# Interleaving the high and low half of each weight block in the expert matmuls of a hybrid decoder layer

## What is computed

```python
def expert(acc, prm):
    wg, wu, wd, gt = prm
    hid = jax.nn.silu(h @ wg) * (h @ wu)
    return acc + gt[:, None] * (hid @ wd), None

out, _ = lax.scan(expert, jnp.zeros_like(h), (w_gate, w_up, w_down, gates.T))
```

## Time and profile before

| | us |
|---|---|
| median of 3 runs | 792.75 (791.99 to 793.56) |
| span of the profiled execution | 794.2 |
| PE busy in it | 728.8 (92%) |
| PE weight loads | 570.3 (72%) |
| DVE busy | 636.6 (80%) |
| ACT busy | 526.4 (66%) |
| POOL busy | 307.2 (39%) |

### The profile page before, as it was taken

One profiled execution on the slowest core, in us unless ns is written; L12 is line 12 of the kernel. 1 busy time (PEld: TensorE's weight loads), 2 busy tenths in 40 slices (PEclk: granted clock), 3 DMA queues, 4 the chain that ended last, 5 costly groups with the idle time before them and its releaser, 6 DMA issues.

```text
span 794.2 us, 12672 instructions
## 1 busy us (share of the span) xinstructions
PE 728.8 (92%) x4733; PEld 570.3 (72%) x4734; DVE 636.6 (80%) x538; ACT 526.4 (66%) x544; POOL 307.2 (39%) x214
## 2 busy tenths in 40 slices
PE   3669999989679999999999999999999999999980
PEld 1248577544457888888888888888888888888860
DVE  3363294635648999999999999999999999999973
ACT  2020133455527887888888888878888888888761
POOL 7300000040053456654456644566544566544000
PEclk9979999999659999999999999999999999999996
DMA  8999987710528899999999999999999999999501
GB/s 337 357 405 379 367 313 275 292 69 0 212 76 309 319 383 378 372 367 370 383 379 364 377 371 372 381 381 369 372 373 381 365 383 369 371 375 372 202 0 61
DMA packets 102004, 249.78 MB, mean 315 GB/s; under 512 B 8134, under 2 KB 8146, under 8 KB 98898
## 3 DMA queue, kind: packets, MB, share of 16 engines
q1 hardware_dynamic: 96448, 244.33, 82.9%
q10 hardware_dynamic: 5092, 3.46, 1.4%
q0 software_dynamic: 432, 1.59, 0.6%
HBM read 248.30 MB, written 1.07 MB: 314 GB/s over the span
## 4 chain that ended last, share of the span: by engine, by line
PE 84%; DVE 5%; DMA 4%; POOL 2%; ACT 2%; issue 2%; ACTq 0%; DVEq 0%; POOLq 0%
PE PS L1250 45%; PE PS L1238 8%; PE PS L1218 7%; PE PS L1209 6%; PE PS L1042 5%; PE PS L1160 3%; PE PS L1036 3%; POOL line L373 2%; DMA toe<-line_dram 2%; PE PS L1228 1%; DMA tabT<-in_rel_bias_dram 1%; PE PS L1017 1%; DVE MOD L698 1%; DVE S L774 1%; DVE S L754 1%
## 5 line engine op out<-in xcount | busy, mean ns | idle before, releaser
L918 DVE TENSOR_TENSOR WL<-W,WH 128x2048 fp32r<-128x2048 f32 x187 | 419.8, 2295 | 7.1 <-ACT WH L619 7.1
L619 ACT CAST WH<-W 128x2048 fp32r<-128x2048 f32 x187 | 349.9, 1903 | 48.6 <-PE PS L1250 48.6
L416 POOL TENSOR_SCALAR OG<-slot_no,cur 128x128 f32<-128x128 f32 x64 | 161.7, 2531 | 0.0
L1250 PE MATMUL PS<-WH,XT 128*128 128x512 f32 x512 | 140.2, 396 | 0.6 <-DVE XT L928 0.6
L1250 PE MATMUL PS<-WL,XT 128*128 128x512 f32 x508 | 140.0, 397 | 0.0
L403 POOL COPY cur<-PG 128x4 f32 (+1 forms) x33 | 8.3, 251 | 274.8 <-PE PS L1228 227.3
L1250 PEld LDWEIGHTS PS<-WH,XT 128*128 128x128 f32 x512 | 97.0, 190 | 23.8 <-DVE XT L928 0.6
L1250 PEld LDWEIGHTS PS<-WL,XT 128*128 128x128 f32 x508 | 96.0, 189 | 22.4
L413 POOL TENSOR_SCALAR OH<-slot_no,cur 128x128 bf16<-128x128 f32 x64 | 106.5, 1674 | 0.0
L1250 PE MATMUL PS<-WH,HT 128*128 128x512 f32 x256 | 70.5, 398 | 1.5 <-issue 1.5
L698 DVE SCALAR_TENSOR_TENSOR MOD<-W,cS,MOD 128x2048 f32<-128x2048 f32 x20 | 46.9, 2347 | 30.1 <-DMA W<-in_w_ada_dram 29.8
(11 more groups left out here) (184 smaller groups left out, 762.3 us busy)
## 6 DMA issues: line engine op xcount, KB each, us to landing
W<-in_w_gate_dram SPq DMA_DIRECT2D x64, 1024.0 KB, 8.0
W<-in_w_down_dram SPq DMA_DIRECT2D x64, 1024.0 KB, 6.2
W<-in_w_up_dram SPq DMA_DIRECT2D x63, 1024.0 KB, 9.9
W<-in_w_ada_dram SPq DMA_DIRECT2D x24, 1024.0 KB, 8.1
W<-in_w_in_dram SPq DMA_DIRECT2D x12, 1024.0 KB, 13.2
W<-in_w_out_dram SPq DMA_DIRECT2D x4, 1024.0 KB, 11.6
toe<-line_dram POOLq DMA_DIRECT2D x1, 1536.0 KB, 14.5
X<-in_x_dram ACTq DMA_DIRECT2D x1, 1024.0 KB, 12.4
```

The costliest lines, as they stand in the source:

```text
L416: nc.gpsimd.tensor_scalar(OG[:, buf, t, :], slot_no[:], cur[:, buf, 0, t:t + 1], cur[:, buf, 1, t:t + 1], ALU.is_equal, ALU.mult).then_inc ...
L619: nc.scalar.copy(WH[:, (UPE * odd + u) % SPLITS, :], source).then_inc(hi_ready, 1)
L918: nc.vector.tensor_tensor(low, source, WH[:, (UPE * odd + u) % SPLITS, :].bitcast(f32), ALU.subtract).then_inc(lo_ready, 1)
L1250: last = nc.tensor.matmul(PS[:, bank, :], lhsT, w[:, q * 512:(q + 1) * 512], start=begin, stop=end)
```

## The change

In `unit` both waits, on `hi_ready` and on `lo_ready`, now stand ahead of the first matmul. The loop over the four blocks is now outside, and the loop over the high and the low half inside: the block from WH and the same block from WL follow each other, and both go past the same stationary block. The matmuls are the same in number, shape and destination. The last one still raises `split_used`. Nothing on ACT, DVE, POOL or SP changes.

```diff
                 def unit(n, at, spare, outs):
 
-                    for high in (True, False):
-                        pe.wait_ge(hi_ready if high else lo_ready, n + 1)
-                        w = WH[:, at % SPLITS, :] if high else (HnL if spare else WL[ring_slot(0, at)])[:]
-                        for q in range(4):
+                    pe.wait_ge(hi_ready, n + 1)
+                    pe.wait_ge(lo_ready, n + 1)
+                    for q in range(4):
+                        for high in (True, False):
+                            w = WH[:, at % SPLITS, :] if high else (HnL if spare else WL[ring_slot(0, at)])[:]
                             bank, lhsT, begin, end = outs(q, high)
                             last = nc.tensor.matmul(PS[:, bank, :], lhsT, w[:, q * 512:(q + 1) * 512],
                                                     start=begin, stop=end)
```

## The result

The changed kernel takes 815.64 us (815.14 to 817.90) against 793.15 us (791.99 to 794.59) for the kernel before, four runs each: a ratio of 1.028, with a 95% interval of 1.025 to 1.031. It is 22.5 us slower; 20.2 us had been forecast. The profiled execution has a span of 813.6 us. The kernel before was run again beside the experiments, with medians of 793.35 us (e1 to e4) and 794.49 us (e5 to e7); the ratios given with them are to those runs, and are not the plain quotients of the medians.

A forecast was written before the change was run, and what follows sets the result against it. PE was taken as the bound, with DVE close behind; 0.69 + 0.07 - 0.12 = 0.64 us a turn over 31 turns, plus 0.36, gave 20.2 us on the 792.75 us median: 813.0 us, range 809 to 822.

The forecast's parts named there:

- What bounds the kernel, and where: Expert pass: PE busy throughout each 16.82 us turn, DVE nearly so; moving the wait costs 0.64 us a turn at unit 3.
- the cover of unit 3: Unit 3's four high-half matmuls, under which DVE finishes the low half, 0.69 us after PE has started the unit.
- The delay stays: DVE's next start follows PE's end of unit 3 by a slackless 3.33 us chain, so the offset returns every turn.
- The hand-over: Time from DVE's end of unit 3's low half to PE's load: taken as 0.07 us, bounds 0.05 and 0.23.
- The catch-up: Unit 3 after its wait: first four loads take 0.76 us and not 0.88, giving back 0.12 us; other bound nothing.
- The last expert's unit 5: `hidden(31)` stands ahead of its low half, so PE waits there: 0.41 + 0.07 - 0.12 = 0.36 us, once.
- Sharing a stationary block: High and low matmuls on one stationary block: saves between nothing and 0.01 us per four matmuls; taken as nothing.
- The extra wait ahead of a unit: Second wait before each unit's first load: made good by PE's queue; at unit 4 perhaps a few hundredths of a microsecond.
- The wait paid once: Rival: DVE gains 0.64 us on PE in the first turn and keeps it; 793.4 us, no change; chance 0.03.
- the fall of the clock: Rival: PE's new idle time each turn lowers its clock, 31 x 1.6 = 50 us more, 863 us; chance 0.05.
- the gain from shared blocks: Rival: wait paid once and matmuls shorter, up to 0.12 us a turn, 3.7 us in all; 789.7 us; chance 0.03.
- The sum: Whole kernel: 31 x 0.64 = 19.8, and 0.36: 20.2 us slower, 813.0 us for the median.

The follow-up runs named there:

- e1: Changed kernel with the old matmul order (four blocks from WH, then four from WL), both waits still ahead of the unit: 816.85 us, ratio to before 1.029.
- e4: Changed kernel, PE's code untouched, with unit 3's high half made ahead of YH on ACT and its low half ahead of YL on DVE: 797.34 us, ratio 1.0035.
- e5: Changed kernel with unit 3's halves made ahead of YH and YL, and only the wait on `lo_ready` ahead of a unit: 793.60 us, ratio 0.9996.
- e7: Kernel before, PE's order and waits kept, with only unit 3's halves made ahead of YH and YL: 794.38 us, ratio 1.0002.
- two single-part runs: e1, the moved wait without the new matmul order, 816.85 us; and e2, the new order without unit 3's moved wait, 794.55 us.
- e2: Changed kernel, but unit 3 and the last expert's unit 5 keep the old order and old place of the wait: 794.55 us, ratio 1.001.
- e6: Changed kernel with only the wait on `lo_ready` ahead of a unit, ACT and DVE in their old order: 813.78 us, ratio 1.024.

## Why the prediction was right

- *What bounds the kernel, and where.* Right. PE was the bound by its busy time, with DVE close behind; the cover of unit 3 was the place. The wait occurs at unit 3 in 31 turns and at unit 5 of the last expert, and nowhere else is a low half waited for. The two single-part runs show the wait to be the whole cost and the order to be none of it.
- *The delay stays.* Right. The loop as now measured over turns 3 to 28: DVE's start to the end of unit 3's low half 11.93 us (11.90 forecast), hand-over 0.12 (0.07), load of unit 3 to ACT's copy 2.16 (2.16), copy to DVE's next start 3.33 (3.33); 17.53 us in all against 17.46.
- *The hand-over* is the term that was mis-sized most. The bounds were 0.05 and 0.23 us, and I took 0.07 on the ground that the load would carry the wait. With two waits ahead of the load only one of them rides on it in this trace, and the one on the low half is an instruction of its own (L1246, 51 ns): 0.12 us. With one wait it is 0.05 us. That is 0.05 us a turn, 1.5 us of the 2.3 us that the forecast fell short of. DVE's part, 0.02 us longer, is 0.7 us more.
- *The catch-up* after a wait was right: 0.34 us from the first load to the second matmul against 0.46 in the stream, 0.12 us.
- *The last expert's unit 5* was put at 0.36 us and cost 0.41: its second matmul starts at 790.24, and one distance of 0.23 after another from 789.37 would have had it at 789.83.

```profile
789.37 0.40 PE L1251 MATMUL PS<-WL,HT 128*128 128x512 f32 x1
...
790.24 0.39 PE L1251 MATMUL PS<-WL,HT 128*128 128x512 f32 x1
```

- *Sharing a stationary block.* Right in that it saves nothing that counts: 4734 loads as before. In the five kernels with the alternating order in which no wait falls inside a unit (after, e2, e4, e5, e6) the mean distance between two matmuls of a unit is 230.7 to 231.9 ns, for 231.9 before, hence at most 1.2 ns a matmul. The scatter was not the only such pair in the kernel before: in units 4 and 5 two blocks in a row already share their stationary block (`k = 2 * (u - 4) + q // 2`), and the distance inside such a pair is no shorter there (232.5 ns on the mean, 232.1 from one pair to the next). The 216 ns that the Trainium skill gives in "TensorE: Matmul & The Clock Gate" ("Back-to-back issue gap"), as the isolated gap of a matmul of 512 columns, were not reached by any of the five, and the 131 ns that it gives there for a sustained stream less still; the distance after the first matmul of a pair is the same as after the second, within 1 ns.
- *The extra wait ahead of a unit* "may add a few hundredths of a microsecond, which end in the wait at unit 3". Both halves hold: it is 0.08 us at unit 4, unseen in the changed kernel, and it showed as soon as the wait at unit 3 was removed.
- *The rivals.* The wait paid once is refuted by the even turns; the fall of the clock did not come (1.00 through the turns); the gain from shared blocks is bounded above.
- *The sum.* 31 x 0.716 + 0.41 = 22.6 us, for 22.5 measured. The interval of the ratio stands for 19.8 to 24.4 us, so that an agreement within 0.1 us is luck; what the terms are worth is known from the traces.
- *One reading was wrong, without effect.* The prediction puts the profiled span of 794.2 us 1.45 us above the median of the runs. But the median is of launch times, which are longer than the span: 815.3 us for a span of 813.6 in the profiled execution of after. By that difference of 1.7 us the profiled execution of the kernel before lay nearly 3 us above the median, an estimate. The forecast for the median does not use the difference.

## What to carry to other kernels

When a step that was interleaved with its inputs is changed to need all inputs at its start, look up for each instance when the last input arrives and compare it with the start of the step, not with its present use: here five of six units had margins of 0.84 us and more, and the sixth had none. Then ask whether the engine that is late gets its own next start from the engine that now waits; if it does, the delay is paid in every turn, however idle the late engine becomes. A second wait ahead of an instruction is not free where the engine is late already: here it cost 0.06 us at unit 3 and 0.08 us at unit 4. Wait on the one semaphore that implies the other.

## What the hardware showed beyond that

With unit 3's low half ahead of YL, POOL's OG instructions (L416) took 3.81 us on the mean in place of 2.75, and POOL was busy for 113 us in ten turns in place of 92. POOL's work is the same; what changed is what DVE does beside it, four low halves in a row in place of three. From 300 to 700 us, first in the kernel before and then in the same kernel with the low half sooner:

```profile
L416 POOL TENSOR_SCALAR OG<-slot_no,cur 128x128 f32<-128x128 f32 x48 | 131.7, 2747 | 0.0
```

```profile
L416 POOL TENSOR_SCALAR OG<-slot_no,cur 128x128 f32<-128x128 f32 x48 | 182.6, 3808 | 0.0
```

The mean hides that only one of the two OG of a turn takes longer. Here are both, with DVE's last subtraction in the row, first in the kernel before:

```profile
418.24 4.71 POOL L416 TENSOR_SCALAR OG<-slot_no,cur 128x128 f32<-128x128 f32 x1
420.08 2.28 DVE L918 TENSOR_TENSOR WL<-W,WH 128x2048 fp32r<-128x2048 f32 x1
422.94 0.79 POOL L416 TENSOR_SCALAR OG<-slot_no,cur 128x128 f32<-128x128 f32 x1
```

and with the low half sooner:

```profile
416.01 6.83 POOL L416 TENSOR_SCALAR OG<-slot_no,cur 128x128 f32<-128x128 f32 x1
420.05 2.28 DVE L918 TENSOR_TENSOR WL<-W,WH 128x2048 fp32r<-128x2048 f32 x1
422.83 0.78 POOL L416 TENSOR_SCALAR OG<-slot_no,cur 128x128 f32<-128x128 f32 x1
```

The first OG starts while DVE subtracts and ends 0.59 us after the last one in the row (422.95 against 422.36), or 0.51 us after it (422.84 against 422.33) where there are four in a row; this is so in all 24 turns from 300 to 700 us of both kernels. The second one, beside DVE's YL, takes 0.78 to 0.79 us, as each of two of them did near the start of the pass, where DVE makes no subtraction:

```profile
229.96 1.57 POOL L416 TENSOR_SCALAR OG<-slot_no,cur 128x128 f32<-128x128 f32 x2
```

So POOL is not slowed down by a factor. An OG that starts beside the subtractions of 128x2048 is held until they are over, and the more of them are in the row, the longer it takes. The second OH (L413, 0.60 us by itself) takes 2.98 us, from 415.28 to 418.26, and ends 0.39 us after the first subtraction (415.58 to 417.87), although the next one has begun; why it gets through between two and OG does not is not shown, nor was it tested whether a shared way to the memory is what holds them. It cost nothing here, as POOL has idle time in each turn, but it would in a kernel where POOL is close to the path.
